# Reading a regrouped block back from DRAM as two transfers of two column chunks each, and signalling the matmul operand in twos

## The reference

```python
for i in range(DEPTH):                       # DEPTH = 2
    u = rmsnorm(h, norm_mix[i])
    if i % 2 == 0:
        m = conformer_conv_module(u, ...)    # 2048->4096, GLU, causal conv 31, rmsnorm, silu, 2048->2048
    else:
        m = short_gated_conv(u, ...)         # 2048->6144, conv 3 between two gates, 2048->2048
    h = h + m
    h = h + squared_relu_mlp(rmsnorm(h, norm_mlp[i]), mlp_w1[i], mlp_w2[i])   # 2048->8192->2048
    h = h + per_layer_embedding(h, p[i], norm_ple[i], ple_w_proj[i], ple_w_gate[i])
return rmsnorm(h, norm_final)
```

## Time and profile before

| what | us |
|---|---|
| median of three runs | 2269.68 |
| lowest and highest of them | 2267.79, 2270.37 |
| the profiled execution | 2267.54 |
| its span, first to last instruction | 2265.8 |
| TensorE busy in the span | 2244.1 (99%) |
| DVE busy | 1430.2 (63%) |
| ACT busy | 1122.8 (50%) |
| the 56 reads of `staged` into `xt`, issue to landing, median | 3.3 |

### The profile page before, as it was taken

One profiled execution on the slowest core, in us unless ns is written; L12 is line 12 of the kernel. 1 busy time (PEld: TensorE's weight loads), 2 busy tenths in 40 slices (PEclk: granted clock), 3 DMA queues, 4 the chain that ended last, 5 costly groups with the idle time before them and its releaser, 6 DMA issues.

```text
span 2265.8 us, 29642 instructions
## 1 busy us (share of the span) xinstructions
PE 2244.1 (99%) x10210; PEld 1867.2 (82%) x10210; DVE 1430.2 (63%) x1625; ACT 1122.8 (50%) x1393; POOL 146.7 (6%) x185
## 2 busy tenths in 40 slices
PE   8999999999999999999999999999999999999998
PEld 7998688888888888888888888888888888888886
DVE  6998776645545555667766667666455556556665
ACT  4545655534534534556644444555345345345555
POOL 2777100000000000000000000000000000000000
PEclk9999999999999999999999999999999999999999
DMA  9444377766856756777776777777668567666873
GB/s 342 157 149 149 120 264 221 252 200 195 267 186 204 249 200 213 227 242 241 230 233 207 238 241 214 264 219 252 200 195 265 189 204 248 202 216 212 271 241 111
DMA packets 493952, 494.58 MB, mean 218 GB/s; under 512 B 257920, under 2 KB 296000, under 8 KB 493120
## 3 DMA queue, kind: packets, MB, share of 16 engines
q1 hardware_dynamic: 492336, 491.83, 67.4%
q10 hardware_dynamic: 1408, 0.89, 0.1%
q0 software_dynamic: 144, 1.05, 0.1%
HBM read 460.16 MB, written 33.55 MB: 218 GB/s over the span
## 4 chain that ended last, share of the span: by engine, by line
PE 95%; issue 2%; DVE 1%; DMA 1%; ACT 1%; ACTq 0%; SPq 0%; POOL 0%; DVEq 0%; POOLq 0%
PE acc L424 28%; PE acc L426 28%; PE acc L425 28%; PE acc L486 5%; PE acc L496 1%; PE acc L497 1%; PE acc L495 1%; DMA staged<-prows 0%; DMA work<-in_cf_b_pw 0%; PE acc L558 0%; PE acc L557 0%; PE acc L556 0%; DMA pT<-staged 0%; DVE tp L1153 0%; ACTq L700 0%
## 5 line engine op out<-in xcount | busy, mean ns | idle before, releaser
L902 DVE TENSOR_TENSOR wlo<-raw,whi 128x1024 fp32r<-128x1024 f32 x728 | 880.2, 1221 | 581.9 <-ACT whi L578 580.0
L578 ACT ACTIVATE whi<-raw 128x1024 fp32r<-128x1024 f32 x728 | 761.9, 1057 | 769.0 <-PE acc L426 768.8
L424 PE MATMUL acc<-whi,b_hi 128*128 128x512 f32 x1632 | 636.0, 390 | 2.4 <-DVE b_lo L999 1.3
L426 PE MATMUL acc<-whi,b_lo 128*128 128x512 f32 x1632 | 635.3, 389 | 0.0
L425 PE MATMUL acc<-wlo,b_hi 128*128 128x512 f32 x1632 | 635.3, 389 | 0.0
L424 PE MATMUL acc<-whi,a_hi 128*128 128x512 f32 x1280 | 498.4, 389 | 0.3 <-DVE a_lo L993 0.3
L426 PE MATMUL acc<-whi,a_lo 128*128 128x512 f32 x1280 | 498.3, 389 | 0.0
L425 PE MATMUL acc<-wlo,a_hi 128*128 128x512 f32 x1280 | 498.2, 389 | 0.0
L424 PEld LDWEIGHTS acc<-whi,b_hi 128*128 128x128 f32 x1632 | 306.4, 188 | 68.7 <-DVE b_lo L999 1.7
L426 PEld LDWEIGHTS acc<-whi,b_lo 128*128 128x128 f32 x1632 | 306.4, 188 | 63.6
L425 PEld LDWEIGHTS acc<-wlo,b_hi 128*128 128x128 f32 x1632 | 306.4, 188 | 63.3
(11 more groups left out here) (157 smaller groups left out, 1204.1 us busy)
## 6 DMA issues: line engine op xcount, KB each, us to landing
raw<-in_mlp_w SPq DMA_DIRECT2D x256, 1024.0 KB, 5.6
raw<-in_sc_w_in SPq DMA_DIRECT2D x48, 1024.0 KB, 5.8
raw<-in_cf_w_pw SPq DMA_DIRECT2D x64, 512.0 KB, 8.7
raw<-in_ple_w_gate SPq DMA_DIRECT2D x32, 1024.0 KB, 6.0
staged<-prows SPq DMA_DIRECT2D x240, 128.0 KB, 3.3
pT<-staged SPq DMA_DIRECT2D x56, 512.0 KB, 3.3
raw<-in_cf_w_pw SPq DMA_DIRECT2D x16, 1024.0 KB, 7.6
raw<-in_sc_w_out SPq DMA_DIRECT2D x16, 1024.0 KB, 7.4
```

What stands on the lines that cost most here:

```text
L424: nc.tensor.matmul(o, xhi[:, k, s], hi, start=first and c == 0, stop=False)
L426: mm = nc.tensor.matmul(o, xlo[:, k, s], hi, start=False, stop=last and c == 1)
L578: nc.scalar.activation(whi[:, e % SLOTS, :, :], raw[:, e // 2, 2 * (e % 2):2 * (e % 2) + 2, :], ACT.Copy).then_inc(hi_ready, 1)
L902: nc.vector.tensor_tensor(wlo[:, e % SLOTS, :, :], raw[:, e // 2, 2 * (e % 2):2 * (e % 2) + 2, :], whi[:, e % SLOTS, :, :].bitcast(F32), A ...
```

## The change

1. Each of the 56 reads of `staged` into `xt` is issued as two transfers, chunks 0 and 1 of both token halves and then chunks 2 and 3. Each moves 256 KB in runs of 1 KB (256 numbers), where one moved 512 KB in runs of 4 KB. The first raises `xt_ready`, the second a new semaphore, `xt_rest`.
2. With a gain, ACT waits for `xt_rest` ahead of its third chunk; DVE raises `operand_ready` after its second and its fourth chunk.
3. Without a gain, ACT waits for both ahead of its one instruction, and DVE raises `operand_ready` by 2.
4. In `short_out` DVE waits for `xt_rest` ahead of its second pair.
5. TensorE waits for the operand ahead of each half of a unit's first block, and the starts of its counts are doubled.

```diff
@@ -271,6 +271,7 @@
         res_ready = sem("res_ready")
         tp_done, operand_ready = sem("tp_done"), sem("operand_ready")
         tr_ready, staged_ready, xt_ready = sem("tr_ready"), sem("staged_ready"), sem("xt_ready")
+        xt_rest = sem("xt_rest")
         xhi_ready, y_ready = sem("xhi_ready"), sem("y_ready")
         ss_ready, junk_written = sem("ss_ready"), sem("junk_written")
 
@@ -302,6 +303,14 @@
 
         @block.sync
         def _(sp):
+            staged_cols = staged.rearrange("p (m c n) -> p m c n", m=2, c=4)
+            xt_by_cols = xt.rearrange("p (m c n) -> p m c n", m=2, c=4)
+
+            def fetch():
+                for i, landed in enumerate((xt_ready, xt_rest)):
+                    nc.sync.dma_start(xt_by_cols[:, :, 2 * i:2 * i + 2, :],
+                                      staged_cols[:, :, 2 * i:2 * i + 2, :]).then_inc(landed, 16)
+
             def tile(b, q, src):
 
                 sp.wait_ge(lo_ready, HALVES * b - HALVES + 2 * q + 2)
@@ -329,7 +338,7 @@
 
                 def back():
                     stage(r.T)
-                    nc.sync.dma_start(xt, staged).then_inc(xt_ready, 16)
+                    fetch()
                 return back
 
             def load_unit(unit, w, before, col=0, row=0):
@@ -426,18 +435,18 @@
                         mm = nc.tensor.matmul(o, xlo[:, k, s], hi, start=False, stop=last and c == 1)
                 mm.then_inc(half_used, 1)
 
-            def multiply(b, a, pair, xin, ready=None, each=2):
+            def multiply(b, a, pair, xin, ready=None):
 
                 xhi, xlo = xin
                 if not (isinstance(a, int) and a < 2):
                     pe.wait_ge(acc_free, a - 1)
                 for e in range(HALVES):
-                    if ready and e % each == 0:
-                        pe.wait_ge(ready[0], ready[1] + e // each + 1)
+                    if ready:
+                        pe.wait_ge(ready[0], ready[1] + e + 1)
                     half(b, e, pair, xhi, xlo, (2 * e, 2 * e + 1), e == 0, e == HALVES - 1)
 
-            def multiply_unit(unit, xin, ready, each=2):
-                multiply(unit.b, unit.a, 0, xin, ready, each)
+            def multiply_unit(unit, xin, ready):
+                multiply(unit.b, unit.a, 0, xin, ready)
                 with pe.Fori(1, BLOCKS) as j:
                     multiply(unit.b + j, unit.a + j, j % 2, xin)
 
@@ -447,9 +456,9 @@
                 by = distance(up[0], up[1])
                 multiply_unit(up[0], X[u], ready)
                 with pe.Fori(0, GROUPS - 1) as g:
-                    multiply_unit(down[0].shifted(by, g), X[hid], (operand_ready, up[0].shifted(by, g).o))
+                    multiply_unit(down[0].shifted(by, g), X[hid], (operand_ready, 2 * up[0].shifted(by, g).o))
                     multiply_unit(up[1].shifted(by, g), X[u], None)
-                multiply_unit(down[-1], X[hid], (operand_ready, up[-1].o))
+                multiply_unit(down[-1], X[hid], (operand_ready, 2 * up[-1].o))
 
 
             pe.wait_ge(const_ready, 3)
@@ -529,21 +538,21 @@
                                               wproj[:, l, c, j * NB:(j + 1) * NB], start=c == 0, stop=c == 1)
                 mm.then_inc(emb_done, 1)
 
-            multiply_unit(pw2, X[1], (y_ready, 0), 1)
-            multiply_mlp(0, 0, (operand_ready, pw2.o))
-            multiply_unit(gate[0], X[0], (operand_ready, mlp[0][1][-1].o))
-
-            multiply(win.b, win.a, 0, X[1], (operand_ready, gate[0].o))
+            multiply_unit(pw2, X[1], (y_ready, 0))
+            multiply_mlp(0, 0, (operand_ready, 2 * pw2.o))
+            multiply_unit(gate[0], X[0], (operand_ready, 2 * mlp[0][1][-1].o))
+
+            multiply(win.b, win.a, 0, X[1], (operand_ready, 2 * gate[0].o))
             multiply(win.b + 1, win.a + 1, 1, X[1])
             multiply(win.b + 2, win.a + 2, 2, X[1])
             with pe.Fori(1, BLOCKS) as j:
                 for part in range(3):
                     multiply(win.b + 3 * j + part, win.a + 3 * j + part, part, X[1])
 
-            multiply_unit(wout, X[0], (y_ready, UNITS), 1)
-            multiply_mlp(1, 1, (operand_ready, wout.o))
+            multiply_unit(wout, X[0], (y_ready, UNITS))
+            multiply_mlp(1, 1, (operand_ready, 2 * wout.o))
             g1 = gate[1]
-            multiply(g1.b, g1.a, 0, X[1], (operand_ready, mlp[1][1][-1].o))
+            multiply(g1.b, g1.a, 0, X[1], (operand_ready, 2 * mlp[1][1][-1].o))
             with pe.Fori(1, BLOCKS - 1) as j:
                 multiply(g1.b + j, g1.a + j, j % 2, X[1])
 
@@ -629,10 +638,13 @@
 
                 act.wait_ge(xt_ready, 16 * x + 16)
                 if gain is None:
+                    act.wait_ge(xt_rest, 16 * x + 16)
                     nc.scalar.activation(by_halves(dst[0])[:, bass.ds(4 * j, 4), :, :], xt_cols,
                                          ACT.Copy).then_inc(xhi_ready, 1)
                     return
                 for c in range(4):
+                    if c == 2:
+                        act.wait_ge(xt_rest, 16 * x + 16)
                     nc.scalar.activation(
                         by_halves(dst[0])[:, bass.ds(4 * j + c, 1), :, :], xt_cols[:, c:c + 1, :, :], ACT.Copy,
                         scale=vec[:, bass.ds(4 * j + c, 1), gain]).then_inc(xhi_ready, 1)
@@ -990,17 +1002,18 @@
 
                 if gain is None:
                     dve.wait_ge(xhi_ready, xh + 1)
-                    last = nc.vector.tensor_tensor(by_halves(dst[1])[:, bass.ds(4 * j, 4), :, :], xt_cols,
-                                                   by_halves(dst[0])[:, bass.ds(4 * j, 4), :, :].bitcast(F32),
-                                                   ALU.subtract)
+                    nc.vector.tensor_tensor(by_halves(dst[1])[:, bass.ds(4 * j, 4), :, :], xt_cols,
+                                            by_halves(dst[0])[:, bass.ds(4 * j, 4), :, :].bitcast(F32),
+                                            ALU.subtract).then_inc(operand_ready, 2)
                 else:
                     for c in range(4):
                         dve.wait_ge(xhi_ready, xh + c + 1)
-                        last = nc.vector.scalar_tensor_tensor(
+                        low = nc.vector.scalar_tensor_tensor(
                             by_halves(dst[1])[:, bass.ds(4 * j + c, 1), :, :], xt_cols[:, c:c + 1, :, :],
                             vec[:, bass.ds(4 * j + c, 1), gain],
                             by_halves(dst[0])[:, bass.ds(4 * j + c, 1), :, :].bitcast(F32), ALU.mult, ALU.subtract)
-                last.then_inc(operand_ready, 1)
+                        if c % 2:
+                            low.then_inc(operand_ready, 1)
 
             def inverse_root(n, total, m, y, t):
 
@@ -1267,6 +1280,8 @@
                 y3_cols = y3.rearrange("p c (m n) -> p c m n", m=2)
                 for i in range(2):
                     c = slice(2 * i, 2 * i + 2)
+                    if i:
+                        dve.wait_ge(xt_rest, 16 * (win.x + j) + 16)
                     nc.vector.tensor_tensor(y3_cols[:, c], xt_cols[:, c], y3_cols[:, c], ALU.mult).then_inc(y3_ready, 1)
                 for i in range(2):
                     dve.wait_ge(xhi_ready, win.xh + 2 * j + i + 1)
```

## The result

The changed kernel takes 2274.48 us (median of 14 runs, 2272.03 to 2276.88), the kernel before in the same sessions 2269.57 (14 runs, 2267.68 to 2272.26). By the medians it is **4.9 us slower**, outside the range of the prediction; the ratio on record is 1.0024, 95% interval 1.0017 to 1.0031, which is 3.9 to 7.0 us. The profiled execution has a span of 2271.3 us, where the earlier trace rows had 2265.8.

The account below looks back on a forecast made before the run. TensorE was taken to bound the kernel, busy 2244.1 of 2265.8 us. Gate to win -1.3 and hidden boundaries +0.9, others zero, gave -0.4: 2269.68 to 2269.3 us, no measurable change; range 2266.6 to 2273.0.

Parts of the forecast that it names:

- Where there is anything to win: At gate to win, half 6: first pair lands 0.49 us sooner, 1.3 us won; four other gain boundaries win nothing.
- The forecast's own lower case: At gate to win: if the first transfer landed no sooner than the whole read, 0.85 us would still be won.
- The bound of 1.6 us on all waiting: TensorE, 300 to 2250 us: busy for 1948.43 of 1950 us, so at most 1.6 us of waiting could be won.
- When the two transfers land: Reads of `staged`: the whole block lands 0.65 us later than one read, half the mean of L355's pairs.
- d: Delay of the whole block landing in two transfers against one read: taken as 0.65 us, bounds 0 and 1.8.
- The hidden boundaries: Eight hidden-to-down boundaries: ACT waits for both transfers, the whole delay goes into half 6, 0.9 us lost.
- rival 2: Second transfer held up by weight tiles, half 6 late at all eight down units: 7.3 us more, 2277.0; chance 0.05.
- The weight tiles: Loads of tiles 1 to 3 start some 0.4 us later; no split shows a wait for a tile: zero cost.
- Waits added on TensorE: 52 more waits at odd halves of 13 first blocks: taken as 0, upper bound 0.5 us in all.
- the other boundaries with a gain: Four boundaries besides gate to win show no wait, so sooner signals and a later second transfer: zero both ways.
- rival 1: Late blocks, but covered: reads behave as L355's pairs, lost 4.2, won 1.3, 2.9 us more, 2272.6; chance 0.23.
- The rule: Skill's rule against splitting into partition halves: second transfer brings only its issue, block's end comes later, never sooner.

Follow-up runs that it names:

- the kernel with signals alone: Changed kernel with one 512 KB read again; with a gain DVE still signals after its second and fourth chunk: 2268.57 us, -0.7 against the kernel before.
- the kernel with the split and pairs: Changed kernel, but after hidden blocks too ACT starts on the first landed pair of chunks and DVE signals each pair: 2267.78 us, -0.7 against the kernel before.
- the kernel split only after hidden blocks: Changed kernel with only the 32 reads after hidden blocks in two transfers, the others one: 2275.02 us, +5.6 against the kernel before.
- the one split only with a gain: Changed kernel with the read after hidden blocks one transfer again, the other 24 still split: 2270.11 us, +0.7 against the kernel before.

## Why the prediction was wrong

*Where there is anything to win.* Right in size: 1.3 us of waiting at gate to win was forecast to go, and it went (1.56 with the slow restart). But the first pair came 0.17 us sooner than one read, not 0.49. The forecast's own lower case, 0.85 from the signal alone, is the nearer one: the kernel with signals alone won 0.7. That nothing at all is left of the wait is luck, since the read was issued 0.94 us earlier in its block; in the kernel with the split and pairs it was issued 0.3 us earlier, and 0.3 us stayed lost. The bound of 1.6 us on all waiting was too low, because busy time hides 0.16 us of each gap and the slow restart: 1.56 + 0.56 = 2.1 were lost in that stretch.

*When the two transfers land.* **This step failed, by its size.** I took d = 0.65, half of what the pairs of L355 showed, because the new runs are longer. Measured, d is 1.24: the pairs' own mean, not halved. The argument by run length was wrong in kind. At 4 KB in two the block was as late as at 1 KB, and at 2 KB nearly on time. I also took 0.35 us for the second issue from the earlier trace rows; it takes 0.61, the first takes 0.56, and in the one window looked at the first data start 0.45 us later than before. The 0.44 us that I read as L355's issue is no issue's time either: the first of each pair took 0.37 or 0.38 us, the second 0.51. That showed that an issue's length is not fixed.

*The hidden boundaries.* Right in mechanism, and rival 2 names it. For d of 1.25 the sum gave 4.2 us; 5.06 was measured. Six new stops at 0.11 us of slow restart account for 0.7 of the difference; that term was missing, though the earlier trace rows had the gap of 1.67 us beside a wait of 1.29. The rest is within the scatter of single landings (3.0 to 5.4 us for L311): in the kernel split only after hidden blocks, the same boundaries lost 6.9 us.

*The weight tiles.* **This step failed too.** "No split shows a wait for a tile" held for the kernel before and I took it for a wide margin. It was not: the tiles are issued right behind the read, 11 us into a block, and after the change ACT waits for one at 18 places (none before, two to four in the three kernels with one read). In pw2 this reaches TensorE, for 1.4 us at blocks 2 and 3 of this execution. The split that waits for tile 1 of block 2 is

```profile
294.27 1.06 ACT L587 ACTIVATE whi<-raw 128x1024 fp32r<-128x1024 f32 x1 [2.61 <-DMA raw<-in_cf_w_pw]
```

and it stands ahead of the handling of block 1's result, so that and the splits 3 and on, which half 3 waits for, come 1.7 us later than before, 0.3 to 0.4 of which the stop at block 1 had already brought. It does not always come to this: the kernel with the split and pairs lost nothing at these blocks, the one split only with a gain lost 0.64 and 0.80. Elsewhere the four slots took nearly all of it up, as the same kernel with the split and pairs shows: it has 14 such waits, and no stop beyond pw2 costs it more than 0.3 us.

*Waits added on TensorE, the other boundaries with a gain.* Right: zero. Signals alone cost nothing.

*The rivals.* The time is between rival 1 (2272.6) and rival 2 (2277.0). The late block is rival 1's, at its size of d; that ACT's one instruction waits for it and half 6 with it is in both. Whether the weight tiles hold the second transfer up, as rival 2 has it, stays open. I gave the two 0.28 together.

*The rule.* The Trainium skill (DMA: Bandwidth & Descriptors, "Rules for kernel authors") has it that two transfers to disjoint partition halves serialize and that one transfer is to be preferred. The run by partition halves agrees and goes further: the two were 1.4 us later than the one, at the same bytes. The fit of 2.0 us plus bytes in the Trainium skill (same page, "Anatomy of one DMA") is given there for transfers that GpSimd issues, which the prediction did not say; those here are SP's. Its estimate of 2.6 us for 256 KB was too low for them: no landing of L311 took less than 3.0 us.

## What to carry to other kernels

Before splitting a transfer to start its reader sooner, look at every reader: the one that still waits for all of it pays the delay of the last part, and here seven of the eight places had 0.4 to 1.3 us to spare and one had none. Signal by parts behind one transfer first; that won 2.8 us here (0.5 to 4.5), and the split on top of it won nothing. When a nearby row shows the cost of the same shape of edit, take it as it stands rather than scale it by a property whose effect no row shows.

## What the runs showed that I had not expected

- The time to issue a transfer on SP depends on its shape and on whether another was issued just before: 0.348 us for 128 x 1024 numbers; for two in a row 0.349 and 0.433 (128 x 512), 0.482 and 0.597 (64 x 1024), 0.565 and 0.613 (128 x 2 x 256). A median over both kinds names a time that no issue took. In the one pair of windows looked at, the data of a read start 0.45 us later with a first issue 0.22 us longer.
- Two reads of 64 partitions each were as slow as two with runs of 1 KB (+11.7 and +11.5 us), two of 128 partitions and 2 KB only +2.1.
- After the stops of 0.1 us and more listed here TensorE's second matmul starts 0.31 to 0.34 us after the first, not 0.23: about 0.11 us more to each stop.
- A 1 KB transfer issued behind each read, 56 times, changed nothing that can be measured.
